# The shifted load of the values in three pieces, and the finished stick-breaking heads turned six steps after their norm

## The chip, the cores and the metric

The kernel runs on one core of a Trainium2 chip. The metric is device time in microseconds of one launch, as the median of three runs. Profiles come from one more execution, taken by the hardware profiler; times in it are counted from the start of its span.

## What is computed

Two blocks in sequence on x of 2048 positions by 1024 features, all in float32. The first block is a projection, three mixers (spatial gating, convolution, a gated recurrence), a projection back and a layer norm. The second block is the one that matters here:

```python
def second_block(x, ...):
    h = rmsnorm(x, norm1_g); p = h @ w_in            # u | dq dk dv | sq sk sv
    a_out = pool_mixer(u, pool_w, pool_scale)
    b_out = diff_attention(dq, dk, dv, lam, ...)     # 4 heads, 2 softmax maps of 64 each
    c_out = stick_breaking_attention(sq, sk, sv, g)  # 4 heads of 64
    x = x + concat(a_out, b_out, c_out) @ w_out
    h2 = rmsnorm(x, norm2_g)
    x = x + (silu(h2 @ w_gate) * (h2 @ w_up)) @ w_down
    return rmsnorm(x, final_norm_g)

# stick-breaking, strictly causal (s < t):
# beta[t,s] = sigmoid(q.k/8);  A[t,s] = beta[t,s] * prod_{s<j<t} (1 - beta[t,j]);  o = rmsnorm(A v) * g
```

Since A[t,s] is the difference of two neighbouring running products, A v can be computed as running products times the differences of neighbouring rows of v. For this the kernel needs v and v shifted by one position.

## The kernel before

The sequence is worked in two halves (hf = 0, 1) of 1024 positions. In each half come the first block, then the second block's projections, its attention, its output projection and its feed-forward part. Large products are done as three float32r products of high and low parts (lines 1411 to 1413). All five engines run programs made from one list, PLAN, which a planner (`weave`) writes in advance; each engine works off its own steps strictly in that order, and so does SyncE (SP), which issues nearly all DMAs.

Queries, keys and values are spilled to HBM as they are projected (`spill_qk`, `spill_v`: q_scr, k_scr, v_scr) and loaded back by unit. There are six units per half, u = 0 to 5: two of stick-breaking (two heads each), then four of softmax differences. The last spilled values are those of projection dv1. The step `attend` makes ScalarE and VectorE wait until all staged data are spilled, since the attention's rows take their place; the first sigmoid stands behind it.

`attend` then goes through steps x: for stick-breaking one step for each unit, block of 128 queries (i = 0 to 7) and head (hh), so unit 0 has steps 0 to 15 and unit 1 has steps 16 to 31; softmax units have eight steps each. In a step TensorE computes the scores of x, and turns and multiplies the attention rows of step x - LV (LV = 5 in the first half and 3 in the second). Scores of a stick-breaking step: ScalarE takes the sigmoid (line 2023), VectorE the running product (`scan`, line 2632).

The values of a stick-breaking unit are loaded twice: line 2970 loads v into `UV`, lines 2976 and 2977 load the shifted v into `UVS` (`uv_shifted`). On 128 partitions position = 128 n + p, so shifting by one position is: partitions 1 to 127 from rows 0 to 126, and partition 0 from row 127 of the tile before. Both units share one UVS; the second unit's shifted load waits for the first's difference. GpSimd subtracts (`differences`, lines 2893 to 2904, planned at steps 0 and 6), and TensorE's first product with the values of a unit waits for that (`shifted`). In SyncE's order, unit 0's shifted load is followed by loads of wo, the spills of q3, k3 and dv1, and then the loads of unit 1.

When four query blocks of both heads are complete (g = 0, 1), `norm_heads` evacuates them, `back` turns them on TensorE, and `norm` emits `o_norm`: a sum on VectorE, then an eps-add, a power and a scaling on GpSimd (a_hi_p). `flip` turns the result on TensorE into feature rows (lines 1726 to 1731), and ScalarE and VectorE evacuate it as high and low parts (lines 2070 and 2651) into the operand of the output projection, which begins after the attention. `flip` is put on a list with the step from which it is due:

```python
tail.append((now[0] + 3, flip))     # line 1208
```

At the end of each step the due entries are emitted in every engine's order. If a flip's input isn't ready when TensorE gets there, TensorE waits, with all that is behind it.

Of the kernel before, what the change touches and what calls it, by code (L numbers as in the profile page):

```python
# [169 lines left out]
def build(nc, xt, xr, w1, wo1, w2, wo2, wgu, wd, rep, par, sgu_t, lam, masks, rows, out):  # L170
# [3 lines left out]
    up, at, new = tally.up, tally.at, tally.new  # L174
# [92 lines left out]
    UVS = sb("uv_shifted", [16, 128], W0 + 40960)  # L267
# [47 lines left out]
    vsc = nc.dram_tensor("v_scr", [6, 128, 16, 128], F32, kind="Internal").ap()  # L315
# [700 lines left out]
    def plan_attention(hf, env):  # L1016
# [47 lines left out]
        now = [0]  # L1064
# [132 lines left out]
        def norm(st, g, o, a):  # L1197
            u, x = st["u"], st["u"] % 2
            emit("o_norm", hf, st, g, o, a, used.get(("us", x, g), []))
            used["us", x, g] = [("o_normed", hf, u, g)]  # L1200

            def flip():
                b = tbank()
                emit("flip", hf, st, g, o, b, grab(BK[b]))
                BK[b].free = [("mix_lo", hf, u, g)]
                settle.append((now[0] + 1, (st["mt"], g), ("mix_lo", hf, u, g)))
                used["oraw", x, g] = [("flip", hf, u, g)]
            tail.append((now[0] + 3, flip))

        def attend():  # L1210
            while "dense2" not in env:
# [1479 lines left out]
    def gpsimd(pool):  # L2691
# [9 lines left out]
        for kind, *a in PLAN:  # L2701
# [88 lines left out]
            elif kind == "conv_hist":  # L2790
                hf, = a
# [67 lines left out]
            elif kind == "pool_sum":  # L2859
                hf, j = a  # L2860
                e = PX[0]
                for mark in new("pool", [("proj", hf, 1, 7, 1)]):
                    pool.wait_ge(*at(*mark))
                if j:
                    for mark in new("pool", [("pooled", hf, 0), ("pool_hist", hf, 0)]):
                        pool.wait_ge(*at(*mark))
                if hf:
                    for mark in new("pool", [("pool_hist", 0, j)]):
                        pool.wait_ge(*at(*mark))
                else:  # L2870
                    for mark in new("pool", [("zeros",)]):
                        pool.wait_ge(*at(*mark))
                copy(e[:, 0:15], PH[:, j, :]).then_inc(*up("pool_head", hf, j))
                for mark in new("pool", [("evac", hf, f"2u{j}", 1), ("pool_head", hf, j)]):
                    pool.wait_ge(*at(*mark))
                copy(PH[:, j, :], e[:, 1024:1039]).then_inc(*up("pool_hist", hf, j))

            elif kind == "combine":
                hf, st = a
                p, L = st["p"], 128 * st["n"]  # L2880
                ra, rb = st["ra"][:, 0:L], st["rb"][:, 0:L]
                for mark in new("pool", [("inverse", hf, st["x"])]):
                    pool.wait_ge(*at(*mark))
                pool.tensor_scalar(RLS[:, p, 2:3], LS[:, p, 0:1], RLS[:, p, 1:2], NLAM[:, 0:1], op0=ALU.mult, op1=ALU.mult
                                   ).then_inc(*up("weight", hf, st["x"]))
                for mark in new("pool", [("weight", hf, st["x"])]):
                    pool.wait_ge(*at(*mark))
                pool.tensor_scalar(rb, rb, RLS[:, p, 2:3], 0.0, op0=ALU.mult, op1=ALU.add).then_inc(
                    *up("weighted", hf, st["x"]))
                for mark in new("pool", [("weighted", hf, st["x"])]):  # L2890
                    pool.wait_ge(*at(*mark))
                tt(ra, ra, rb, ALU.add).then_inc(*up("attn", hf, st["x"]))
            elif kind == "differences":
                hf, u = a
                nt = 8 * hf + 8
                if u == 0:
                    for mark in new("pool", env_free(hf)):
                        pool.wait_ge(*at(*mark))
                    pool.memset(UVS[0:1, 0, :], 0.0).then_inc(*up("first_zero", hf))
                    for mark in new("pool", [("first_zero", hf)]):  # L2900
                        pool.wait_ge(*at(*mark))
                for mark in new("pool", [(f"ld_v{u % 2}", hf, u), ("ld_before", hf, u, 0), ("ld_before", hf, u, 1)]):
                    pool.wait_ge(*at(*mark))
                tt(UV[u][:, 0:nt, :], UV[u][:, 0:nt, :], UVS[:, 0:nt, :], ALU.subtract).then_inc(*up("shifted", hf, u))
            elif kind == "o_norm":
                hf, st, g, o, _, _ = a
                m, x = 4 if st["kind"] == "d" else 8, st["u"] % 2
                w, ms = 512 // m, slice(m * g, m * g + m)
                for mark in new("pool", [("o_sum", hf, st["u"], g)]):
                    pool.wait_ge(*at(*mark))  # L2910
                rsqrt(UR[:, x, ms], US[:, x, ms], 1.0 / w, 1e-6, "o", hf, st["u"], g)
                for mark in new("pool", [("o_rs", hf, st["u"], g)]):
                    pool.wait_ge(*at(*mark))
                v = o.rearrange("p (n b) -> p n b", b=w)
                tt(v, v, UR[:, x, ms].unsqueeze(2).to_broadcast([128, m, w]), ALU.mult).then_inc(
                    *up("o_normed", hf, st["u"], g))

            elif kind == "out_sq":
                hf, t = a
                for mark in new("pool", [("out_sq", hf, t)]):  # L2920
                    pool.wait_ge(*at(*mark))
                rsqrt(RS[:, t:t + 1], SS[:, t:t + 1], 1.0 / D, 1e-6, "out", hf, t)
            elif kind == "out" and a[1] % 2:
                hf, t = a
                x = XR2[t][:, :]
                if t == 1:
                    for mark in new("pool", [("ld_fg", hf)]):
                        pool.wait_ge(*at(*mark))
                for mark in new("pool", [("out_scaled", hf, t)]):
                    pool.wait_ge(*at(*mark))  # L2930
                tt(x, x, FG[:, :], ALU.mult).then_inc(*up("out_pool", hf, t))


    def sync(sp):
        for kind, *a in PLAN:
# [25 lines left out]
            elif kind in ("load_k", "load_v"):  # L2961
                hf, u, held = a
                nt = 8 * hf + 8
                for mark in new("sp", held):
                    sp.wait_ge(*at(*mark))
                if kind == "load_k":
                    sp.dma_start(f32(UK[u % 2][:, :, 0:128 * nt]), ksc[u, :, :, 0:128 * nt].rearrange("r p c -> p r c")
                                 ).then_inc(*up(f"ld_k{u % 2}", hf, u, by=16))
                else:
                    sp.dma_start(UV[u % 2][:, 0:nt, :], vsc[u, :, 0:nt, :]).then_inc(*up(f"ld_v{u % 2}", hf, u, by=16))  # L2970
            elif kind == "load_before":
                hf, u, held = a
                nt = 8 * hf + 8
                for mark in new("sp", held):
                    sp.wait_ge(*at(*mark))
                sp.dma_start(UVS[1:128, 0:nt, :], vsc[u, 0:127, 0:nt, :]).then_inc(*up("ld_before", hf, u, 0, by=16))
                sp.dma_start(UVS[0:1, 1:nt, :], vsc[u, 127:128, 0:nt - 1, :]).then_inc(*up("ld_before", hf, u, 1, by=16))
            elif kind == "load_q":
                hf, u, c, held = a
                for mark in new("sp", held):  # L2980
                    sp.wait_ge(*at(*mark))
                for r in range(2):
                    for z in range(2):
                        sp.dma_start(f32(UQ[c][64 * z:64 * z + 64, r, :, :]), qsc[
                            u, :, 64 * r:64 * r + 64, 512 * c:512 * c + 512].rearrange("h p c -> p h c")).then_inc(
                            *up(f"ld_q{c}{2 * r + z}", hf, u, by=16))
            elif kind == "load_fg":
                hf, = a
                for mark in new("sp", [("wino", hf, 10, 1, "b22")]):
                    sp.wait_ge(*at(*mark))  # L2990
                sp.dma_start(FG[:, :], rep[4]).then_inc(*up("ld_fg", hf, by=16))
            elif kind == "out":
                hf, t = a
                if t % 2:
                    for mark in new("sp", [("out_pool", hf, t)]):
                        sp.wait_ge(*at(*mark))
                else:
                    for mark in new("sp", [("out_dve", hf, t)]):
                        sp.wait_ge(*at(*mark))
                sp.dma_start(out[hf * T + 128 * t:hf * T + 128 * t + 128, :], XR2[t][:, :]).then_inc(  # L3000
                    *up(f"st_out{t}", hf, by=16))
# [100 lines left out]
```

## Time and profile before

| | before |
|---|---|
| median of 3 runs | 3786.78 us (3783.37 to 3788.77) |
| profiled execution | 3790.2 us, its span 3788.4 us |
| mean granted clock of TensorE | 0.971 |
| TensorE busy | 3528.9 us, 93% |
| GpSimd, VectorE, ScalarE busy | 46%, 57%, 30% |
| DMA | 275.81 MB, mean 73 GB/s |
| attention, first half | about 760 to 990 us |
| attention, second half | about 2519 to 3000 us |

Busy times of the engines overlap, so they do not add up to the span. TensorE is the engine to follow; idle time on another one matters only where TensorE waits behind it. The granted clock is given in tenths or hundredths of full speed: 1.00 is 2.4 GHz and 0.50 is 1.2 GHz.

### The profile page before, as it was taken

Reading aid. Unit: us, or ns where it says so; the run is one execution under the profiler, and the core shown is the slowest. Engines: PE = TensorE matmul, PEld = TensorE weight load, DVE = VectorE, ACT = ScalarE, POOL = GpSimd, SP = SyncE. Lnnn points to the kernel's source line nnn. Section 1 sums busy time; section 2 is a strip of 40 time slices with the busy share of each in tenths; the row PEclk is TensorE's granted clock in tenths of the full one; section 3 lists DMA queues with packets and bytes.
Section 4 is the critical chain, followed back from the end, with each engine's and each line's share of the span. In section 5 each row is a group of like instructions: output and inputs, shape, how many; then the busy total and the mean of one; then the engine's idle time right before and its main releaser. Section 6 shows DMA issues by size and latency. Waiting matters only on the chain.

```text
span 3788.4 us, 51922 instructions
## 1 busy us (share of the span) xinstructions
PE 3528.9 (93%) x22042; PEld 2945.7 (78%) x22042; DVE 2147.5 (57%) x2745; ACT 1155.1 (30%) x1919; POOL 1730.2 (46%) x1248
## 2 busy tenths in 40 slices
PE   7989999969999999999899999959999999999998
PEld 6878878857777787877778888757788787878876
DVE  7754576346355545456874466627777446454545
ACT  2122112247322322223122122316666322222223
POOL 4232433518445646455333323621388336555455
PEclk9999999989999999999999999989999999999999
DMA  3101412534201111113110132351222211111111
GB/s 121 35 25 33 150 53 84 179 110 133 95 23 40 61 45 56 45 56 138 36 45 29 34 150 78 114 184 58 69 81 70 77 31 42 45 56 56 45 67 62
DMA packets 79569, 275.81 MB, mean 73 GB/s; under 512 B 8937, under 2 KB 9193, under 8 KB 76780
## 3 DMA queue, kind: packets, MB, share of 16 engines
q1 hardware_dynamic: 70696, 242.25, 18.9%
q10 hardware_dynamic: 8642, 30.24, 2.1%
q8 instruction: 174, 2.85, 0.3%
q14 instruction: 57, 0.47, 0.0%
HBM read 224.23 MB, written 48.23 MB: 72 GB/s over the span
## 4 chain that ended last, share of the span: by engine, by line
PE 69%; DVE 16%; POOL 5%; ACT 3%; issue 3%; another core or an unknown queue 3%; DMA 1%; SPq 0%; POOLq 0%; DVEq 0%; ACTq 0%
PE ps L1411 19%; PE ps L1412 18%; PE ps L1413 18%; PE ps L1417 4%; DVE acc L2108 3%; PE ps L1711 2%; PE ps L1681 2%; DVE tf_lo_p L2107 2%; PE ps L1682 2%; DVE af_hi_p L2107 1%; PE ps L1716 1%; ACT wd_hi L1765 1%; DVE af_lo_p L2107 1%; DMA uv_shifted<-v_scr 1%
## 5 line engine op out<-in xcount | busy, mean ns | idle before, releaser
L2692 POOL TENSOR_TENSOR ring_lo<-ring_raw,ring_hi 128x512 fp32r<-128x512 f32 (+1 forms) x356 | 599.2, 1689 | 383.8 <-ACT ring_hi L1765 374.2
L1411 PE MATMUL ps<-a_hi,ring_hi 128*128 128x512 f32 x1472 | 591.2, 402 | 29.0 <-DVE af_hi_p L2107 15.8
L1412 PE MATMUL ps<-a_lo,ring_hi 128*128 128x512 f32 x1472 | 578.9, 393 | 0.0
L1413 PE MATMUL ps<-a_hi,ring_lo 128*128 128x512 f32 x1472 | 578.1, 393 | 0.0
L1411 PEld LDWEIGHTS ps<-a_hi,ring_hi 128*128 128x128 f32 x1472 | 279.4, 190 | 103.7 <-DVE af_hi_p L2107 23.4
L1413 PEld LDWEIGHTS ps<-a_hi,ring_lo 128*128 128x128 f32 x1472 | 279.6, 190 | 60.1
L1412 PEld LDWEIGHTS ps<-a_lo,ring_hi 128*128 128x128 f32 x1472 | 279.5, 190 | 54.6
L2107 DVE TENSOR_TENSOR xres<-xres,ps 128x512 f32<-128x512 f32 x352 | 234.8, 684 | 149.8 <-PE ps L1413 147.8
L1411 PE MATMUL ps<-wd_hi,af_hi 128*128 128x512 f32 x704 | 278.5, 396 | 23.4 <-DVE xres L2107 17.5
L1412 PE MATMUL ps<-wd_lo,af_hi 128*128 128x512 f32 x704 | 277.3, 394 | 0.0
L1413 PE MATMUL ps<-wd_hi,af_lo 128*128 128x512 f32 x704 | 276.9, 393 | 0.0
L1765 ACT ACTIVATE ring_hi<-ring_raw 128x512 fp32r<-128x512 f32 (+1 forms) x286 | 180.5, 635 | 309.5 <-PE ps L1413 195.8
L2693 POOL TENSOR_SCALAR ring_hi<-ring_raw 128x1024 fp32r<-128x1024 f32 x78 | 102.4, 1313 | 368.8 <-PE ps L1413 320.7
L1681 PE MATMUL ps<-uk,uq 128*128 128x512 f32 (+2 forms) x480 | 201.4, 420 | 67.0 <-ACT rowa L2023 37.0
L1411 PE MATMUL ps<-tf_hi,ring_hi 128*128 128x512 f32 x640 | 251.5, 393 | 10.1 <-DVE sl_p L2107 10.1
L1412 PE MATMUL ps<-tf_lo,ring_hi 128*128 128x512 f32 x640 | 251.1, 392 | 0.0
L1413 PE MATMUL ps<-tf_hi,ring_lo 128*128 128x512 f32 x640 | 250.7, 392 | 0.0
L2692 POOL TENSOR_TENSOR ring_lo<-rlf,ring_hi 128x512 fp32r<-128x512 f32 x72 | 96.6, 1351 | 227.1 <-ACT ring_hi L1765 227.0
L2108 DVE SCALAR_TENSOR_TENSOR acc<-hc,par,acc 128x1024 f32<-128x1024 f32 x120 | 194.7, 1638 | 1.8
L2692 POOL TENSOR_TENSOR ring_raw<-ring_raw 128x512 f32<-128x512 f32 x128 | 186.2, 1455 | 10.0
L1411 PEld LDWEIGHTS ps<-wd_hi,af_hi 128*128 128x128 f32 x704 | 134.3, 191 | 54.6 <-DVE xres L2107 19.2
L1682 PE MATMUL ps<-uk,uq 128*128 128x512 f32 (+2 forms) x480 | 175.3, 373 | 0.0
(305 smaller groups left out, 8076.0 us busy)
## 6 DMA issues: line engine op xcount, KB each, us to landing
ring_raw<-w SPq DMA_DIRECT2D x92, 512.0 KB, 3.5
ring_raw<-wgu SPq DMA_DIRECT2D x68, 512.0 KB, 3.7
uq<-q_scr SPq DMA_DIRECT2D x96, 256.0 KB, 5.0
ring_raw<-wd SPq DMA_DIRECT2D x34, 512.0 KB, 3.6
ring_raw<-wo SPq DMA_DIRECT2D x32, 512.0 KB, 3.7
uk<-k_scr SPq DMA_DIRECT2D x6, 2048.0 KB, 10.7
rlf<-wgu SPq DMA_DIRECT2D x20, 512.0 KB, 4.5
xraw<-xt SPq DMA_DIRECT2D x16, 512.0 KB, 7.9
```

The lines of the kernel that those rows point to most:

```text
L1411: pe.matmul(o, ah, bh, start=begin and i == 0, stop=False)
L1412: pe.matmul(o, ah, bl, start=False, stop=False)
L1413: last = pe.matmul(o, al, bh, start=False, stop=end and i == len(pairs) - 1)
L1417: return pe.transpose(o, i, IDF[0:i.shape[0], 0:i.shape[0]])
L1681: pe.matmul(o, Q[:, r, 0, qs], K[:, r, ks], start=True, stop=False)
L1682: t = pe.matmul(o, Q[:, r, 1, qs], K[:, r, ks], start=False, stop=not end)
L1711: t = pe.matmul(PS[b][:, 0:128], ATS[si[0]][:, 128 * k:128 * k + 128], UV[u % 2][:, kk, :], start=kk == 0, stop=kk == n - 1)
L1765: copy = lambda o, i, **k: act.activation(o, i, ACT.Copy, **k)
L2107: tt = lambda o, a, b, op: dve.tensor_tensor(o, a, b, op=op)
L2108: stt = lambda o, a, s, b, op0, op1, **k: dve.scalar_tensor_tensor(o, a, s, b, op0=op0, op1=op1, **k)
L2692: tt = lambda o, a, b, op: pool.tensor_tensor(o, a, b, op=op)
L2693: copy = lambda o, i: pool.tensor_scalar(o, i, 1.0, 0.0, op0=ALU.mult, op1=ALU.add)
```

## The change

The load of partitions 1 to 127 becomes two: partitions 1 to 112 (112 rows) and 113 to 127 (15 rows). The load of partition 0 stays. Each of the three has a semaphore of its own, and `differences` waits for all three. Flips of stick-breaking heads become due six steps after their norm is emitted and not three; those of the softmax heads stay at three.

```diff
@@ norm(), flip
-            tail.append((now[0] + 3, flip))
+            tail.append((now[0] + (3 if st["kind"] == "d" else 6), flip))
@@ gpsimd, differences
-                for mark in new("pool", [(f"ld_v{u % 2}", hf, u), ("ld_before", hf, u, 0), ("ld_before", hf, u, 1)]):
+                for mark in new("pool", [(f"ld_v{u % 2}", hf, u)] + [(f"ld_before{i}", hf, u) for i in range(3)]):
                     pool.wait_ge(*at(*mark))
@@ sync, load_before
-                sp.dma_start(UVS[1:128, 0:nt, :], vsc[u, 0:127, 0:nt, :]).then_inc(*up("ld_before", hf, u, 0, by=16))
-                sp.dma_start(UVS[0:1, 1:nt, :], vsc[u, 127:128, 0:nt - 1, :]).then_inc(*up("ld_before", hf, u, 1, by=16))
+                for i, (p0, p1) in enumerate(((1, 113), (113, 128))):
+                    sp.dma_start(UVS[p0:p1, 0:nt, :], vsc[u, p0 - 1:p1 - 1, 0:nt, :]).then_inc(*up(f"ld_before{i}", hf, u, by=16))
+                sp.dma_start(UVS[0:1, 1:nt, :], vsc[u, 127:128, 0:nt - 1, :]).then_inc(*up("ld_before2", hf, u, by=16))
```

## Rows read from the trace of the kernel before

**Rows 1.** The page: TensorE's busy time, its granted clock by slice, the last chain by engine.
```profile
PE 3528.9 (93%) x22042; PEld 2945.7 (78%) x22042; DVE 2147.5 (57%) x2745; ACT 1155.1 (30%) x1919; POOL 1730.2 (46%) x1248
...
PEclk9999999989999999999999999989999999999999
...
PE 69%; DVE 16%; POOL 5%; ACT 3%; issue 3%; another core or an unknown queue 3%; DMA 1%; SPq 0%; POOLq 0%; DVEq 0%; ACTq 0%
```

**Rows 2.** DMA issues: out<-in, count, KB each, median us from issue to landing.
```profile
uq<-q_scr SPq DMA_DIRECT2D x96, 256.0 KB, 5.0
...
v_scr<-vst SPq DMA_DIRECT2D x12, 512.0 KB, 4.3
...
uv<-v_scr SPq DMA_DIRECT2D x6, 1024.0 KB, 5.3
...
uv_shifted<-v_scr SPq DMA_DIRECT2D x2, 1016.0 KB
```

**Rows 3.** Timeline of SyncE's queue, second half: start, us, line, transfer, count.
```profile
2490.05 0.29 SPq L2976 DMA_DIRECT2D uv_shifted<-v_scr  x1
2490.39 24.62 SPq L2977 DMA_DIRECT2D uv_shifted<-v_scr  x1
...
2533.24 4.54 SPq L2959 DMA_DIRECT2D v_scr<-vst  x2
```

**Rows 4.** Timeline of GpSimd, second half; in brackets the idle time before and its end.
```profile
2541.31 4.50 POOL L2692 TENSOR_TENSOR uv<-uv,uv_shifted 128x2048 f32<-128x2048 f32 x1 [54.81 <-DMA uv_shifted<-v_scr]
```

**Rows 5.** Stretches: length, busy PE, PEld, DVE, ACT, POOL; clock, DMA share, GB/s.
```profile
2495.00:2500.00 5.00, 5.00 (x38) 5.00 (x38) 0.00 (x0) 0.00 (x0) 0.00 (x0) 0.85 1.00 416
2500.00:2510.00 10.00, 10.00 (x86) 10.00 (x85) 0.00 (x0) 1.19 (x2) 0.00 (x0) 1.00 0.07 29
```

**Rows 6.** Timelines of ScalarE and TensorE, second half.
```profile
2552.27 1.28 ACT L2023 ACT_TABLE_LOAD   x1 [33.98 <-DMA v_scr<-vst]
...
2554.64 0.80 PE L1681 MATMUL ps<-uk,uq 128*128 128x512 f32 x1 [35.81 <-ACT rowa L2023]
...
2622.48 0.75 PE L1417 MATMUL ps<-par,a_hi_p 128*128 128x128 f32 x4 [2.33 <-POOL a_hi_p L2692]
```

**Rows 7.** Timeline of ScalarE, first half: its first step of the attention.
```profile
769.96 1.28 ACT L2023 ACT_TABLE_LOAD   x1 [10.23 <-DMA v_scr<-vst]
```

**Rows 8.** Timeline of SyncE's queue, first half.
```profile
759.75 0.81 SPq L2959 DMA_DIRECT2D v_scr<-vst  x2
...
766.07 17.48 SPq L2977 DMA_DIRECT2D uv_shifted<-v_scr  x1
783.64 13.30 SPq L2984 DMA_DIRECT2D uq<-q_scr  x8
```

**Rows 9.** Timeline of GpSimd, first half.
```profile
802.70 2.34 POOL L2692 TENSOR_TENSOR uv<-uv,uv_shifted 128x1024 f32<-128x1024 f32 x1 [40.22 <-DMA uv_shifted<-v_scr]
...
829.36 2.75 POOL L2692 TENSOR_TENSOR ur<-ur,mhalf 128x8 f32<-128x8 f32 x1
```

**Rows 10.** Timeline of TensorE, first half: the instructions after its gaps.
```profile
804.99 0.45 PE L1681 MATMUL ps<-uk,uq 128*128 128x128 f32 x1 [11.62 <-DMA uq<-q_scr]
...
808.33 0.45 PE L1417 MATMUL ps<-par,a_hi_p 128*128 128x128 f32 x1 [1.26 <-POOL a_hi_p L2692]
...
833.37 0.30 PE L1417 MATMUL ps<-par,a_hi_p 128*128 128x128 f32 x1 [3.69 <-POOL a_hi_p L2692]
...
853.23 0.41 PE L1417 MATMUL ps<-par,a_hi_p 128*128 128x128 f32 x2 [2.98 <-POOL a_hi_p L2692]
```

**Rows 11.** Stretches after such gaps, first half; columns as in rows 5.
```profile
805.00:813.00 8.00, 6.74 (x38) 5.70 (x39) 1.40 (x3) 2.60 (x6) 2.94 (x4) 0.50 0.04 16
833.00:837.00 4.00, 3.63 (x22) 2.80 (x22) 2.24 (x2) 2.10 (x3) 0.23 (x1) 0.66 0.00 0
854.00:858.00 4.00, 4.00 (x30) 3.08 (x31) 1.60 (x6) 3.33 (x8) 0.12 (x1) 0.59 0.21 84
```

**Rows 12.** Instructions that touch v_scr, 2480 to 2660: their DMAs' landing.
```profile
DMA to landing us min/median/max: 4.7/17.6/18.3
```

## The prediction

> **What bounds the kernel now.** I read the page first: TensorE is busy for 93% of the span and the chain that ended last is 69% TensorE, so time can only be won where TensorE stands still or runs at its lower clock [rows 1]. The two attention stages are the places to look, because the change touches nothing else. Each starts with two stick-breaking units, u = 0 and 1, which need the shifted values. I then read, in this order, the transfers by line, SyncE's queue at the start of the second half's attention, and the DMA engines by stretch, and last the idle gaps of TensorE itself.
>
> The transfers: 1016 KB of shifted values is about the size of one plain load of the values, 1024 KB, which lands in 5.3 us [rows 2]. The shifted one is issued at 2490.05 [rows 3] and GpSimd, which waits for it, starts at 2541.31 [rows 4]: 51 us, or 20 GB/s. Between 2500 and 2510 the DMA engines are busy for 0.07 of their time, about 1/16, and move 29 GB/s, while just before they were full at 416 GB/s [rows 5]. So the 127 rows go through one engine of 16. It was behind other traffic at first and then worked alone. The reader should see that two things are blocked by this. SyncE's next issue, the one row of line 2977, holds its queue for 24.62 us [rows 3]; and whatever is issued later has a sixteenth of its data behind the backlog of that one engine.
>
> The Trainium skill, page "DMA: Bandwidth & Descriptors", section "Why a DMA increments its semaphore by 16 and not by 1", states the rule: the number of engines is the largest up to 16 that divides the slowest dimensions, so 127 partitions get one engine. The trace agrees, with 0.07 and 29 GB/s [rows 5].
>
> Second half: the last projection (dv1) ends on TensorE at 2518.8, and its values are spilled to v_scr. The attention's first sigmoid waits for that spill, since the rows it writes wait for all that was staged (`attend`). The spill is issued only at 2533.24, because SyncE stood at line 2977 and then had to pass four more groups of transfers [rows 3]. ScalarE idles 33.98 us for it and starts at 2552.27; TensorE idles 35.81 us [rows 6]. This is the largest hole in the stage.
>
> First half: the same with less behind it. ScalarE waits 10.23 us for the spill [rows 7]. Then the second unit's shifted load is issued, and the one row after it blocks SyncE from 766.07 to 783.55 [rows 8]; GpSimd gets the data at 802.70 [rows 9]. The queries of unit 1 are issued at 783.64, behind it on the slow engine. Their share there is 1 MB / 16 = 64 KB, at 29 GB/s 2.3 us, so they land at about 805: TensorE starts at 804.99 after 11.62 us [rows 10]. Three more gaps, 1.26, 3.69 and 2.98 us, wait for GpSimd's a_hi_p: these are flips of finished stick-breaking heads, placed three steps after their norm was asked for [rows 10].
>
> **The change, part by part.** *The load's pieces.* 112 rows are 7 rows on each of 16 engines. 15 rows cost at best 8 KB / 29 GB/s = 0.3 us (one row on each of 15 engines) and at worst 15 x 0.3 = 4.5 us on one engine. I take the first, the 127 rows having shown only that a count without a divisor goes to one engine; at the worst it still ends some 20 us before anyone asks in the second half. The single row, as before. One more DMA issue each time costs SyncE 0.29 us [rows 3], four times, at moments when nothing on the path waits for SyncE: hidden. One more wait on GpSimd: it comes in front of an instruction that waits for the same load anyway, and behind it stand only the norms of heads that are not due for six steps.
>
> What SyncE now does earlier: two loads of wo, and the spills of q3 and k3. In the second half, 1 MB queries, 2 MB keys, 1 MB values, 1 MB shifted, 1 MB wo and 2 MB spills make 8 MB from 2486.3; at 416 GB/s [rows 5] this is 19 us, so over by about 2507, before the spill of dv1 is ready at 2518.3. No weight that dv1 needs is behind it.
>
> *Second half, the spill.* Ready at 2552.27 - 33.98 = 2518.29 [rows 6]; two issues take 0.81 us [rows 8]. Landing: between 4.3, the median of all twelve [rows 2], and the 10.2 that ScalarE waited in the first half, when one engine had a backlog [rows 7]. I take 5, near the median, since the backlog is what goes. ScalarE then starts at 2524.1 instead of 2552.27: **28.2 us**. Before, GpSimd had unit 0's values at 2541.31 + 4.50, earlier than ScalarE's start, so these do not become the next late thing; after, they are there by about 2510.
>
> *First half, the spill.* 769.96 - 10.23 = 759.73 [rows 7], plus 0.8 and 5, is 765.5: **4.4 us**.
>
> *First half, the queries of unit 1.* Their load waits only for the scores of step 7, and they are needed at step 16. One such transfer lands in 5.0 us [rows 2]. Steps 0 to 15 took from 771.2 [rows 7] to 804.99 - 11.62 = 793.4 [rows 10], 22 us, and the later ones are the longer ones, so the nine from step 7 to step 16 leave at least 12 us. All of the gap goes: **11.6 us**. Next late would be a running product of step 14 or 15; TensorE turns those five steps later, so I charge nothing. The keys are issued ahead of the queries and land before them.
>
> *The flips.* Four per half, eight in all. Each is still four transposes, one ScalarE and one VectorE evacuation; nothing is added. They wait for a chain that starts three steps earlier. Its power alone took GpSimd 2.75 us before the 3.69 us gap [rows 9]. Three steps of 22 / 16 = 1.4 us are 4.1 us, and the chain outlasts them by up to 3.69; three steps more are 4.1 us more, which covers it. So 1.26 + 3.69 + 2.98 = **7.9 us** in the first half. In the second half 2.33 us [rows 6]. The last flips move into the steps of the softmax heads; there each holds one of the two turning banks for its two evacuations, as the softmax heads' own flips do. I charge nothing; at most 4 x 1.4 us (one evacuation each on ScalarE and VectorE) would come back.
>
> *The clock.* After each long gap TensorE is granted the lower of its two levels, 1.2 GHz. From 805 to 813 it is 0.50 with 6.74 us busy; 833 to 837 has 0.66, and 854 to 858 has 0.59 [rows 11]. At 2.4 GHz these stretches would be shorter by 3.4, 4 x 0.34 = 1.4 and 4 x 0.41 = 1.6: **6.4 us**, if the gap ahead of each goes. At the two attention starts a gap of about 6 us stays, so I leave the slow restart there as it is.
>
> Sum: first half 4.4 + 11.6 + 7.9 + 6.4 = 30.3; second half 28.2 + 2.3 = 30.5; together 60.8. The profiled execution took 3790.2 us (span 3788.4), so 3729; the median of the runs is 3786.8, 3.4 lower, so I forecast **3726 us**, 1.6% less. What follows the attention (the wo projection and the feed-forward) starts from the attention's end and moves up with it.
>
> **The rivals.** *A: the spill still lands late.* The loads of unit 1 (5 MB in the second half) are issued right behind it, and half of the value transfers of this stretch took 17.6 us or more [rows 12]. With 17.6 instead of 5 the second half wins 15.6 us, the first half none of its 4.4: 3726 + 12.6 + 4.4 = 3743. For it: that row. Against it: then the engines were full and the spill itself was stuck among them; now it goes first. 13%.
>
> *B: more goes.* If the short gap at the two attention starts leaves the higher clock, each start saves about what the restart at 805 costs, 3.4 us [rows 11]; with a spill landing at 4.3 as well and 5 us from engines that no longer stand behind a late flip, 3726 - 6.8 - 1.4 - 5 = 3713. 12%.
>
> *C: the pieces do not spread, or it does not matter.* Then only the flips and their clock remain, 7.9 + 3.0 + 2.3 = 13: 3774. The Trainium skill has a rule that would make this so: "DMA: Bandwidth & Descriptors", section "Rules for kernel authors", says not to bother with two transfers to disjoint halves of the partitions, since both use all 16 engines already. Against it stands that this load used one engine [rows 5]. 3%. That the flips too give nothing: 3784 to 3790, 2%.
>
> *D: slower.* The granted clock. The page shows full clock in nearly every slice [rows 1], and with the pauses gone TensorE works longer without a rest. If the chip granted it 3% less in the stages where it is full (3528.9 us busy), 106 us would come on top: 3726 + 106 = 3832. It decides from 61 / 3529 = 1.7% less clock on. Against it: the long stages without such pauses already have 9s throughout. 2%.
>
> **How the numbers follow.** The forecast has 68%, A 13%, B 12%, C 3% and 2%, D 2%. The forecast's own spread is from the landing (4.3 to 10.2, twice: 1 less or 10 more) and the clock and flip terms in the first half, of which a third may be overlapped (5): 3718 to 3740. With A and B in, the range is 3708 to 3748. Faster by over 0.2% (7.6 us, about what a measurement of this kernel can tell from no change): 95%; within: 3%; slower: 2%.
>
> **What would show it.** Right: a share of the DMA engines well above 0.07 until the shifted load is in, GpSimd's wait for it under 20 us each; line 2977's successor issued in under 2 us; ScalarE's start less than 7 us after the last vst evacuation in both halves; no gap for uq at step 16; no TensorE gap on a_hi_p. Wrong: a spill that still lands 15 us after its issue (A), a gap of TensorE on a DMA or a scan where the queries' gap was, or a mean granted clock under 0.96 (D).

## The result and the profile after

| | before | after |
|---|---|---|
| median | 3785.53 us (4 runs, 3783.37 to 3788.77) | 3724.38 us (4 runs, 3720.22 to 3726.71) |
| ratio | | 0.9837, 95% interval 0.9819 to 0.9854 |
| profiled execution's span | 3788.4 us | 3722.8 us |
| mean granted clock | 0.971 | 0.980 |
| TensorE busy | 3528.9 us, 93% | 3518.2 us, 95% |

The change wins 61 us; 61 had been forecast. SyncE's queue of the changed kernel, second half (start, us, line, transfer, count), answers to [rows 3]:

```profile
2460.92 0.91 SPq L2977 DMA_DIRECT2D uv_shifted<-v_scr  x2
2461.87 0.25 SPq L2978 DMA_DIRECT2D uv_shifted<-v_scr  x1
...
2489.18 0.80 SPq L2959 DMA_DIRECT2D v_scr<-vst  x2
```

The row that held SyncE for 24.62 us is issued in 0.25 us, and the last spill goes out when it is ready. The stretch behind the load (columns as in [rows 5]):

```profile
2466.00:2477.00 11.00, 11.00 (x89) 11.00 (x88) 0.00 (x0) 0.60 (x1) 0.00 (x0) 0.94 1.01 354
2477.00:2488.00 11.00, 11.00 (x94) 11.00 (x93) 0.00 (x0) 1.20 (x2) 4.62 (x1) 1.00 0.54 216
```

In the first 11 us all 16 DMA engines are busy (share 1.01) and in the next 11 about half of the time (0.54), where before one of 16 was, at 0.07 [rows 5]. ScalarE's first step of the second half, and what TensorE starts with after its gap there and in the first half, answer to [rows 6] and [rows 7]:

```profile
2493.98 1.28 ACT L2023 ACT_TABLE_LOAD   x1 [4.82 <-DMA v_scr<-vst]
...
2496.35 0.80 PE L1681 MATMUL ps<-uk,uq 128*128 128x512 f32 x1 [6.66 <-ACT rowa L2023]
...
764.41 0.69 PE L1681 MATMUL ps<-uk,uq 128*128 128x384 f32 x1 [5.82 <-ACT rowc L2023]
```

33.98 us of waiting have become 4.82, and TensorE's 35.81 us gap 6.66. GpSimd still waits for the shifted values, though for less. The first two rows are of the first half, one for each unit (the second answers to [rows 9]), the third is unit 0 of the second half (answers to [rows 4]):

```profile
742.28 2.40 POOL L2692 TENSOR_TENSOR uv<-uv,uv_shifted 128x1024 f32<-128x1024 f32 x1 [16.11 <-DMA uv_shifted<-v_scr]
774.14 3.44 POOL L2692 TENSOR_TENSOR uv<-uv,uv_shifted 128x1024 f32<-128x1024 f32 x1 [29.47 <-DMA uv_shifted<-v_scr]
...
2477.24 4.62 POOL L2692 TENSOR_TENSOR uv<-uv,uv_shifted 128x2048 f32<-128x2048 f32 x1 [19.88 <-DMA uv_shifted<-v_scr]
```

Of the gaps of [rows 10] nothing is left above 1 us until the softmax units: the queries' wait of 11.62 us and the three on a_hi_p are gone.

**Where the time went.** With all the transposes of line 1417 left out, the flips among them, every kernel of the table below runs the same 20378 recorded matmuls in the same order, so the start of the same matmul can be compared. Cut at ten of them, each stretch took, in us, in the profiled execution of each kernel (those of the experiments below are shown beside them):

```
stretch                       before  after  pieces_  flips_  prime_  four_    flip_  act_
                                             only     only    pieces  engines  nine   queue
start to proj. 1 (hf 0)        504.2  502.5   504.1   504.1   503.4   503.0   503.8   502.8
to the end of dv1 (hf 0)       241.8  241.7   241.6   241.7   236.0   238.7   242.4   238.8
attention, first half          200.9  170.9   182.0   189.8   186.9   171.0   170.7   190.1
wo projection (hf 0)           106.0  108.7   106.0   104.6   106.0   107.4   104.8   108.8
feed-forward and first block   803.4  803.7   801.7   801.7   800.3   803.3   799.8   803.4
next stretch (hf 1)            240.8  240.5   240.9   241.1   240.7   240.7   240.7   240.8
next stretch (hf 1)            408.9  408.9   408.8   409.0   408.6   408.9   408.9   408.7
attention, second half         440.2  408.8   408.0   437.3   435.8   410.0   407.7   441.3
wo projection (hf 1)           113.7  109.2   112.0   113.5   109.4   113.5   112.5   112.7
feed-forward (hf 1)            703.7  703.5   704.2   704.3   703.7   704.4   704.3   704.5
```

The first attention stretch is 756.4 to 957.3 before and 754.6 to 925.5 after, the second 2516.4 to 2956.6 and 2487.3 to 2896.0. (The table ahead of the prediction put the ends of the attention at about 990 and 3000; these stretches end at the last products with the values.) They became 30.0 and 31.4 us shorter. What the span lost beyond these 61.4 lies in stretches that the change doesn't touch.

### The profile page after: what moved, and what is told of

It is laid out like the page before. It is cut to its first block, busy times and chain, and to the rows that moved or that the text cites. A ratio compares the mean times of both kernels' runs of the same rounds, so it can differ in the third digit from the quotient of the medians.

```text
span 3722.8 us, 51933 instructions
## 1 busy us (share of the span) xinstructions
PE 3518.2 (95%) x22042; PEld 2937.1 (79%) x22042; DVE 2152.4 (58%) x2745; ACT 1154.7 (31%) x1919; POOL 1738.0 (47%) x1248
## 4 chain that ended last, share of the span: by engine, by line
PE 72%; DVE 17%; ACT 4%; issue 3%; POOL 3%; DMA 0%; POOLq 0%; SPq 0%; DVEq 0%; ACTq 0%
PE ps L1411 19%; PE ps L1412 19%; PE ps L1413 19%; PE ps L1417 4%; DVE acc L2108 3%; PE ps L1711 2%; PE ps L1681 2%; PE ps L1682 2%; PE ps L1716 2%; DVE tf_lo_p L2107 2%; DVE af_hi_p L2107 1%; ACT wd_hi L1765 1%; DVE af_lo_p L2107 1%; PE ps L1486 1%; DVE px L2107 1%
## 5 line engine op out<-in xcount | busy, mean ns | idle before, releaser
L1411 PE MATMUL ps<-a_hi,ring_hi 128*128 128x512 f32 x1472 | 590.9, 401 | 29.4 <-DVE af_hi_p L2107 16.3
## 6 DMA issues: line engine op xcount, KB each, us to landing
uk<-k_scr SPq DMA_DIRECT2D x6, 2048.0 KB, 10.7
```

What stands on the lines that cost most here:

```text
L1411: pe.matmul(o, ah, bh, start=begin and i == 0, stop=False)
```

## The experiments

The theory: 127 rows go through one DMA engine; its backlog and SyncE's held queue delay the last spill and the queries, and the late norms hold TensorE at the flips. Rivals for each part were put beside it. Each ratio is to the kernel before, timed beside the kernel in question.

**One part alone, load.** The changed kernel with

```diff
-            tail.append((now[0] + (3 if st["kind"] == "d" else 6), flip))
+            tail.append((now[0] + 3, flip))
```

> The load in three pieces alone; stick-breaking flips stay three steps after the norm. If the two parts work on separate holes, the load keeps its part and the flips' holes come back: the two gaps on a_hi_p in the first half (3.7 and 3.0 us) with their restarts at the lower clock (1.4 and 1.6 us) and one of 2.3 us in the second, so about 12 us more than the changed kernel: 3736 us, against 3785 before. The 1.26 us gap of the first flip stays away, since GpSimd no longer stands at the shifted load. Rival: the gaps on a_hi_p were all a result of the blocked GpSimd and go with the load; then it is 3724 to 3727.

Measured: 3734.14 us (3729.82 to 3735.6), ratio 0.9863 (0.9849 to 0.9878). The load brings 51 of the 61 us. The gaps of over 1 us in the first half in which TensorE waits for a_hi_p:

```profile
791.83 0.41 PE L1417 MATMUL ps<-par,a_hi_p 128*128 128x128 f32 x2 [3.02 <-POOL a_hi_p L2692]
...
815.92 0.63 PE L1417 MATMUL ps<-par,a_hi_p 128*128 128x128 f32 x4 [3.69 <-POOL a_hi_p L2692]
...
835.79 0.41 PE L1417 MATMUL ps<-par,a_hi_p 128*128 128x128 f32 x2 [2.98 <-POOL a_hi_p L2692]
```

The last two gaps are as before, to the hundredth. The first one did not stay away, as I had expected: it grew from 1.26 to 3.02 us. Three steps are too short for the chain of the norm even when GpSimd is free, and before, the wait for the queries had hidden most of it. In the second half the flips bring nothing in this pair (408.0 against 408.8).

The kernel before shows why the four gaps aren't of one kind. GpSimd's timeline there, the start of the first norm of the first half, and that of the second half with what stands ahead of it:

```profile
805.12 0.20 POOL L2696 TENSOR_SCALAR ur<-us 128x8 f32<-128x8 f32 x1
...
2605.10 4.55 POOL L2692 TENSOR_TENSOR uv<-uv,uv_shifted 128x2048 f32<-128x2048 f32 x1 [59.29 <-DMA uv_shifted<-v_scr]
2609.74 3.66 POOL L2696 TENSOR_SCALAR ur<-us 128x8 f32<-128x8 f32 x1
```

Both norms start right behind a difference that had waited for the shifted load. So before, GpSimd's blocked queue was what these two gaps (1.26 and 2.33 us) ended on. The gap of the second half goes when the load is fast; under the first one the chain itself is too long for three steps as well. The gaps of 3.69 and 2.98 us have nothing to do with the load.

**One part alone, flips.** The kernel before with the new line of the flips.

> The later flips alone, on the kernel before with its load of 127 rows. Adding theory: 1.3 + 5.1 + 4.6 us in the first half and 2.3 in the second go, 3785 - 13 = 3772 us; the wait for the queries at step 16 (11.6 us) and the one for the spill in the second half (34 us) stay as they were. Rival: later flips without the quicker load give nothing, since GpSimd is the late one: 3783 to 3785.

Measured: 3773.61 us (3767.45 to 3776.49, 6 runs), ratio 0.9966 (0.9954 to 0.9978). The adding theory holds within 2 us: 51.0 from the load and 11.5 from the flips make 62.5 where both together give 61. What is counted twice is the second half's gap, which either part removes. The big waits are untouched:

```profile
804.77 0.44 PE L1681 MATMUL ps<-uk,uq 128*128 128x128 f32 x1 [11.55 <-DMA uq<-q_scr]
```

**Pieces with a prime.** The changed kernel with

```diff
-                for i, (p0, p1) in enumerate(((1, 113), (113, 128))):
+                for i, (p0, p1) in enumerate(((1, 114), (114, 128))):
```

> As the changed kernel, but the pieces are 113, 14 and 1 rows. 113 is a prime, 14 is not. If the number of engines is the largest up to 16 that divides the rows, 113 rows go through one engine and everything of the load's part comes back, as with 127 rows: about 3772 us (the flips' part stays), a DMA share of 0.07 in the stretch after the load, ScalarE's wait for the spill in the second half about 30 us. Rival: cutting the load in two DMAs is what helps, whatever the counts: 3724 us.

Measured: 3760.73 us (3757.07 to 3762.83), ratio 0.9935 (0.9919 to 0.995). Cutting alone is not what helps. Who waited for whom in the second half (us in total, times, longest), and a stretch behind the load:

```profile
POOL uv L2692 <- DMA uv_shifted<-v_scr: 107.8, 2, 55.2
...
ACT L2023 <- DMA v_scr<-vst: 31.7, 1, 31.7
```

```profile
2476.00:2486.00 10.00, 10.00 (x86) 10.00 (x85) 0.00 (x0) 1.19 (x2) 0.00 (x0) 1.00 0.11 34
```

One row more in the first piece and the waits are back. The share is 0.11 and 34 GB/s, not 0.07, but far from full. Yet it is 13 us quicker than flips_only, and I had expected the same time. The attention stretches explain 2.9 + 1.5 = 4.4 us of it, which fits 113 rows in place of 127 on the slow engine: ScalarE's wait is 31.7 and not 34.2 us. Most of the rest of the 16.5 us between the two profiled spans lies in two stretches in which both do the same work: 236.0 against 241.7 us ahead of the first attention, 109.4 against 113.5 behind the second. The rows of these two stretches, first of prime_pieces, then of flips_only (columns as in [rows 5]), show a different granted clock, 0.99 against 0.96 and 0.98 against 0.94:

```profile
512.80:748.80 236.00, 220.94 (x1222) 189.31 (x1221) 133.98 (x133) 64.30 (x105) 104.06 (x74) 0.99 0.35 118
2927.20:3036.60 109.40, 98.92 (x521) 83.85 (x520) 36.41 (x43) 25.01 (x42) 32.44 (x28) 0.98 0.22 78
```

```profile
513.40:755.10 241.70, 225.22 (x1222) 192.58 (x1222) 134.75 (x133) 64.22 (x105) 103.96 (x74) 0.96 0.34 115
2938.60:3052.20 113.60, 103.12 (x522) 86.90 (x522) 36.43 (x43) 25.02 (x42) 32.41 (x28) 0.94 0.20 75
```

Why the chip granted more to this kernel, and in all four of its runs (their mean clocks are 0.975 to 0.977, those of flips_only 0.973 to 0.975), is not shown.

**Four engines.** As above, with pieces (1, 125), (125, 128): 124 = 4 x 31 rows and 3 rows.

> As the changed kernel, but the pieces are 124, 3 and 1 rows. By the divisor reading 124 rows go through 4 engines: in the second half 992 KB / 4 = 248 KB each, 8.6 us at 29 GB/s, beside 7 MB / 16 = 440 KB of the other traffic. That is over before the last projection's spill is ready, so nothing of the backlog reaches it: 3724 to 3729 us, ScalarE's wait for the spill still about 5 us, SyncE held for less than 5 us. So the harm would be in the length of one engine's queue and not in missing 16. Rival: anything short of 16 engines holds SyncE up as before, 3740 us or more.

Measured: 3726.26 us (3724.77 to 3730.19), ratio 0.9842 (0.9828 to 0.9857). Four engines do as well as 16, within what can be told apart. ScalarE's wait is a little longer. The load itself is in by 2482.45, 3 us before the spill is ready, but just before the spill four engines of 16 are still at work (share 0.27, 108 GB/s), on what had queued behind the load:

```profile
2480.00:2486.00 6.00, 6.00 (x48) 5.70 (x46) 0.00 (x0) 0.60 (x1) 3.55 (x1) 1.00 0.27 108
```

```profile
2492.56 1.28 ACT L2023 ACT_TABLE_LOAD   x1 [7.08 <-DMA v_scr<-vst]
```

SyncE was held here too: its last two issues of k3's spill took 6.38 us, over the 5 us that I had set as a bound. It cost nothing, as nothing was ready to be issued. These three row counts (127 or 113, 124, 112) fit one reading: the harm grows with the length of the longest engine's queue, and starts only where that queue outlasts the moment when the next transfer is wanted.

**Held queue or backlog.** The changed kernel, but 127 rows again, issued from ScalarE's queue (the first lines stand in ScalarE's program); the single row stays with SyncE, and `differences` waits for these two.

```diff
+            elif kind == "load_before":
+                hf, u, held = a
+                nt = 8 * hf + 8
+                for mark in new("act", held):
+                    act.wait_ge(*at(*mark))
+                act.dma_start(UVS[1:128, 0:nt, :], vsc[u, 0:127, 0:nt, :]).then_inc(*up("ld_before0", hf, u, by=16))
...
-                for i, (p0, p1) in enumerate(((1, 113), (113, 128))):
-                    sp.dma_start(UVS[p0:p1, 0:nt, :], vsc[u, p0 - 1:p1 - 1, 0:nt, :]).then_inc(*up(f"ld_before{i}", hf, u, by=16))
```

> The flips as in the changed kernel, the load in its old shape of 127 rows and 1 row, but the 127 rows are issued from ScalarE's queue, so they use the one engine still, and SyncE is not held. It separates the two harms. If SyncE's blocked queue is the harm, the spill is issued in time and nearly all is won: about 3728 us, ScalarE's wait for the spill under 8 us, GpSimd's waits for the shifted load still 35 to 50 us. Rival: the one engine's backlog alone does it, whatever queue issues: the spill's sixteenth lands after it, ScalarE waits some 20 us in the second half and the queries' gap in the first stays: 3750 us.

Measured: 3777.31 us (3770.22 to 3780.11, 6 runs), ratio 0.9972 (0.9961 to 0.9984). In time the rival holds, and further than I had put it. The second half first: SyncE's queue, then ScalarE's and GpSimd's timelines:

```profile
2505.72 5.86 SPq L2965 DMA_DIRECT2D v_scr<-vst  x2
```

```profile
2544.15 1.28 ACT L2023 ACT_TABLE_LOAD   x1 [38.45 <-DMA v_scr<-vst]
```

```profile
2541.69 4.49 POOL L2698 TENSOR_TENSOR uv<-uv,uv_shifted 128x2048 f32<-128x2048 f32 x1 [67.77 <-DMA uv_shifted<-v_scr]
```

The spill is issued as soon as it is ready, not 15 us late, and ScalarE waits 38.45 us all the same, more than before. What counts here is the work of the one engine. Estimated from the rows: 1016 KB of the load and a sixteenth of the other 7 MB, 448 KB, are 1.46 MB, at 29 GB/s some 52 us from 2473.7 on, so to about 2525. The spill lands at 2544, and its own share, 64 KB, is only 2 us more, so the estimate is 17 us short: the engine moved less than 29 GB/s with both queues on it. How the two shared it is seen between 2510 and 2530, where q10 is ScalarE's queue (packets, MB, share of 16 engines), and in the landing of the two loads of wo that SyncE issued 5 and 6 us after the long load:

```profile
q1 hardware_dynamic: 715, 1.64, 25.4%
q10 hardware_dynamic: 39, 0.32, 4.0%
```

```profile
DMA to landing us min/median/max: 40.1/41.8/43.5
```

The long load moves at 0.32 MB in 20 us, 16 GB/s, and the two loads of wo are in at 2519.1 and 2523.7, some 18 us before it is, at 2541.69. So the engine serves both queues, and SyncE's transfers did pass the long load; the spill was late because it stood last in SyncE's own queue on an engine that now gave this queue only a part of itself. SyncE wasn't quite free either: its issues of the spills ahead took up to 5 us each.

The first half went the other way than the rival has it. The queries of unit 1 were issued at 772.10 and not at 783.64, and there they had little of SyncE's own ahead of them. Their issue to landing, here and in the kernel before:

```profile
uq<-q_scr SPq DMA_DIRECT2D x4, 256.0 KB, 10.7
```

```profile
uq<-q_scr SPq DMA_DIRECT2D x4, 256.0 KB, 19.3
```

The gap for them is gone, with the one engine as loaded as ever. For this wait SyncE's held queue, and the order within it, was a cause of its own. But the first flip, at six steps, now waits for a GpSimd that gets its shifted values only at 805.08, and nothing is won (190.1 us against 189.8 with flips_only):

```profile
810.70 0.66 PE L1417 MATMUL ps<-par,a_hi_p 128*128 128x128 f32 x2 [11.51 <-POOL a_hi_p L2698]
```

**Flips later still.** The changed kernel with nine steps in place of six.

> The changed kernel with the stick-breaking flips nine steps after the norm. With six, no TensorE gap waits for a_hi_p any more, so nothing is left to win: 3724 us. Rival: a later flip also frees ScalarE and VectorE from standing in their queues, and three more steps give 2 to 4 us more.

Measured: 3720.95 us (3716.01 to 3723.04), ratio 0.9824 (0.9807 to 0.984). The intervals of this one and of six steps overlap for the most part. In the attention stretches it differs from six by 0.2 and 1.1 us. Nothing that can be measured is left there.

**The wait that remained.** The two gaps of 5.8 and 6.7 us wait for the last spill. But what the first sigmoids write (rows in other places) doesn't lie where the spilled data lay; the first to write there is the evacuation of finished heads, many steps on. So the wait was moved there:

```diff
-            emit("attend", hf, fd + env["dense2"])
+            emit("attend", hf, fd + env["dense2"][:2])
...
+            if env["dense2"][2:]:
+                emit("staged", hf, env["dense2"][2:])
+                del env["dense2"][2:]
             emit("heads", hf, st, g, b, a)
...
-            elif kind == "attend":
+            elif kind in ("attend", "staged"):
```

> The changed kernel, and the wait for the staged data's spills is moved from the start of the attention to the first evacuation of finished heads, which is the first to write where they lay. The start then waits only for the last projection and the freed ring. If the spill is what the two remaining gaps wait for (5.8 us in the first half, 6.7 in the second), most of them goes; ScalarE's table load (1.3 us) and its first sigmoid remain, some 2.4 us each, and the restart at the lower clock goes with the gap (about 3 us each): 3724 - 3.5 - 4.3 - 5 = 3711 us. Rival: keys or queries, or the scores' pace, end next and the gain is under 5 us: 3720.

Measured: 3717.47 us (3716.86 to 3718.14), ratio 0.9822 (0.9805 to 0.9838). 7 us and not 13. In the second half the stretch is 8.2 us shorter (400.6), as thought: 4.4 us of the gap are gone, 2.23 are left, and behind so short a gap the granted clock stays at the higher level, 1.00, where it was 0.50 behind 6.66 us. The first 6 us behind the gap, with the wait moved and in the changed kernel:

```profile
2488.55:2494.55 6.00, 4.32 (x22) 3.45 (x23) 5.75 (x3) 2.79 (x6) 0.00 (x0) 1.00 0.91 216
```

```profile
2496.35:2502.35 6.00, 5.16 (x14) 3.94 (x14) 5.11 (x2) 2.01 (x4) 0.00 (x0) 0.50 1.03 300
```

In the first half it is 172.3 us, no better than 170.9: a new wait took the place.

```profile
769.30 0.77 PE L1684 MATMUL ps<-uk,uq 128*128 128x512 f32 x1 [5.52 <-DMA uq<-q_scr]
```

These are unit 0's queries of blocks 4 to 7, whose place is free only when the last projection is done, and which are issued behind its spill.

**Queries before the spill.** On top of that, the last spill is planned after these queries.

```diff
-            emit("spill_v", hf, name, u0)
+            if name != "dv1":
+                emit("spill_v", hf, name, u0)
...
+            while ("q", 0, 1) not in loaded:
+                yield False
+            emit("spill_v", hf, "dv1", 4)
             N = len(steps)
```

> On top of late_spill_wait, whose first half shows a gap of 5.5 us in which TensorE waits for unit 0's second block of queries, issued right behind the spill of the last values: here that spill is issued after these queries, since nothing waits for it now for many steps. The queries' four DMAs then go out 0.8 us earlier and have 1 MB (2.5 us at 416 GB/s) less ahead of them: 3717 - 3 = 3714 us. Rival: their own four issues and landing set the gap, and it stays: 3717.

Measured: 3714.78 us (3712.41 to 3716.57), ratio 0.981 (0.9795 to 0.9825). The wait shrinks by 3.7 us, and the first attention stretch is 168.0 us:

```profile
764.96 0.47 PE L1688 MATMUL ps<-uk,uq 128*128 128x512 f32 x1 [1.82 <-DMA uq<-q_scr]
```

This is the fastest kernel of the study, some 10 us below the changed one.

## Why the prediction was right, point by point

**The load and its rule.** Right. The prime pieces show that the count decides and not the cutting, and four engines show that 16 are not needed. The page "DMA: Bandwidth & Descriptors" of the Trainium skill, section "Why a DMA increments its semaphore by 16 and not by 1", has the rule by which 113 rows get one engine and 124 rows four; the traces agree, with a DMA share of 0.11 and ScalarE's wait of 31.7 us for 113 rows, and 0.27 and 7.08 us for 124. Its advice against splitting a transfer, in "Rules for kernel authors", assumes halves that use all engines; that isn't the case here, and 51 us say so.

**Two things blocked.** Half wrong. I took SyncE's held queue for a harm of its own in both halves. act_queue shows that for the spill of the second half it is none: the spill then goes out in time and lands later still, behind the work of the one engine. For the queries of unit 1 in the first half it is one: issued earlier from a queue without the long load in it, they land in time. That load then keeps GpSimd from the first norm, so freeing SyncE alone gives nothing in sum. The forecast was not touched by this, as the change removes both.

**The spill.** Second half: 28.2 us were forecast. TensorE's gap shrank by 29.15 us, ScalarE's wait by 29.16. First half: 4.4 forecast, 5.4 measured in both. ScalarE waited 4.8 us for it, not 5.8 (two issues and 5).

**The queries, the first flip and the restart behind them.** 11.6 + 1.3 + 3.4 = 16.3 us. Ahead of these gaps the same matmul came 7.1 us earlier than before, and behind them (start 814.15 before, 790.48 after) 23.7: 16.5.

**The two other flips and their restarts.** 5.1 and 4.6 us. The steps in the comparison are 5.8 and 5.0, but 1.3 and 0.8 us were given back in between, where the moved flips now stand, and 0.7 behind the last. Of these 2.7 us some 0.4 for each of the three is the flip's own four transposes, which only changed places. The rest, about 1.5 us, is what can be put down to the term for moved flips, which I had set at nothing with up to 5.6 us as its bound. Altogether the first half gave 30.0 us, for 30.3 forecast.

**The second half's flip.** 2.3 us forecast, with the wrong cause. There the later flips alone took 2.9 us off the stretch (440.2 to 437.3), but with the load already in pieces nothing (408.0 and 408.8). The prediction had all four gaps wait for a chain too long for three steps; this one waited for a GpSimd that stood at the shifted load until 2605.10. The size was right all the same, since the change removes the gap either way. Altogether the second half gave 31.4 us, for 30.5 forecast.

**The rivals.** A (the spill lands late): no, 4.8 us. B (more goes): no. In the second half the first 6 us behind the start were granted 0.50 before and after; in the first half 0.61 before and 0.74 after, so a little of it went there. C: refuted by prime_pieces and flips_only taken together; its price for the flips alone, 3774 us, is what flips_only took. D (a lower clock from denser work): no; the mean rose from 0.971 to 0.980.

**One expectation of the profile missed.** I had GpSimd's waits for the shifted load under 20 us; two are 29.47 and 31.4 us. They begin when GpSimd has nothing else to do, and end 10.7 us after the issue at 763.41 and 18.7 after that at 2494.60; TensorE has no gap behind either. The idle time was a poor thing to name; the landing would have been the right one.

**Around it.** The profiled executions differ by 65.6 us, the medians by 61.2. The rest is in stretches with unchanged work, above all the last wo projection, 113.7 against 109.2 us. It has the same gap of 4.28 us in both, but another clock behind it. The 20 us behind that gap:

```profile
2978.69:2998.69 20.00, 18.11 (x96) 15.65 (x97) 3.34 (x5) 3.26 (x6) 0.00 (x0) 0.77 0.17 53
```

```profile
2918.13:2938.13 20.00, 18.11 (x121) 16.42 (x122) 3.99 (x5) 4.09 (x8) 0.00 (x0) 0.92 0.17 53
```

The first is the kernel before, the second the changed one, which gets through 121 matmuls in the time of 96. Over the eight profiles of the table this stretch takes 109.2 to 113.7 us without order, so it is no effect of the change.

## What to carry to other kernels

Look at the share of the DMA engines while a transfer is waited for: 0.07 means one of 16, and a row count without a good divisor is the likely reason; cutting off a few rows so that the rest divides costs one issue of less than 1 us. Then follow the work of the longest engine to whoever issues next: the price lies in the transfers behind it, here above all a spill and a load of queries. Another queue for the long load brought nothing in sum here (3777.31 us): it let the queries pass, but not the spill, which had much queued ahead of it on the same engine, and the load's own user still waited. When a wait goes, ask whether it was needed at that place at all (7 us here, by waiting for the spill where its memory is first written), and which transfer is next in line. And a wait of one engine for another (TensorE for GpSimd) can have its cause one step further back: look at what the other one was waiting for.

## What the runs showed of the hardware

A late sixteenth counts like the whole. In act_queue the spill went out from another queue than the long load, in time, and ScalarE still waited 38.45 us for it: the two queues share one DMA engine. Neither has it to itself: the long load moved at 16 GB/s beside the other queue, where it moved at 29 GB/s alone in the kernel before [rows 5], and loads of wo issued 5 us after it landed 18 us before it.

A short gap can leave TensorE's clock alone. In the second half's first attention steps the granted clock was 0.50 behind a gap of 6.66 us and 1.00 behind one of 2.23 us.

The same work behind the same gap takes different times. In the 20 us after a gap of 4.28 us, with unchanged instructions, the granted clock was 0.77 in one execution and 0.92 in another, and the stretch differed by 4.5 us. Differences of that size between two single profiles say nothing about a change.
